# Third layer's norm, turn and rotation jobs inside its input tiles, a spare bank for the third up tile, and ScalarE copying both turned halves in the differential attention

## The reference, cut to what matters

```python
def diff_attn(q, k, v, lam):                       # layers 1 and 2 (first_block)
    s = jnp.einsum("bqhmd,bkhmd->bhmqk", q, k) * (B_QK_DIM ** -0.5)
    p = jax.nn.softmax(s, axis=-1)
    a = p[:, :, 0] - lam * p[:, :, 1]
    return jnp.einsum("bhqk,bkhd->bqhd", a, v)

def project(t):                                    # layer 3, in _even_mixer (second_block)
    qa, ka, va, qb, kb, vb = jnp.split(t @ w_in, EVEN_SPLITS, axis=-1)
    return (_rms_norm(_heads(qa, 8, 64), q_gain), _rms_norm(_heads(ka, 2, 64), k_gain), _heads(va, 2, 64), ...)
    # then qa = _rope(qa, cos, sin); ka = _rope(ka, cos, sin)

def _conv_ffn(h, w_up, conv_w, conv_b, w_down):    # all four layers (layers 1 and 2: conv_ffn)
    gate, val = jnp.split(h @ w_up, 2, axis=-1)
    gate = conv(gate, conv_w, width 3, per channel) + conv_b
    return (jax.nn.silu(gate) * val) @ w_down
```

## Time and profile before

| | us |
|---|---|
| median of 3 runs | 3829.44 (3820.06 to 3830.59) |
| profiled execution | 3837.57 |
| its span | 3835.8 |
| TensorE matmuls busy | 3506.9 (91%) |
| VectorE busy | 2035.1 (53%) |
| ScalarE busy | 1306.4 (34%) |
| POOL busy | 410.5 (11%) |

### The profile page before, as it was taken

The page is one execution under the profiler, slowest core; times in us unless marked ns, Lnnn a source line. Parts: engine busy times, 40 slices in busy tenths (PEclk is TensorE's granted clock), DMA queues, the critical chain, the costliest instruction groups (busy, mean ns, idle before and its releaser), DMA issues.

```text
span 3835.8 us, 47682 instructions
## 1 busy us (share of the span) xinstructions
PE 3506.9 (91%) x19065; PEld 2828.1 (74%) x19065; DVE 2035.1 (53%) x3250; ACT 1306.4 (34%) x1977; POOL 410.5 (11%) x351
## 2 busy tenths in 40 slices
PE   6997889999989888999997879899999879989998
PEld 5875678888868666787785547788888656667886
DVE  3655455635546655868413674474454355554354
ACT  4224332212233333323222552531221535434233
POOL 2003430000000140000001471000000013300000
PEclk8997889999999889999997999999999889999999
DMA  5430033434422102555320002134343211113332
GB/s 183 132 111 17 9 83 99 135 95 126 128 60 65 33 18 88 179 156 183 95 64 25 11 20 62 58 124 121 105 129 91 47 31 30 39 50 93 98 98 75
DMA packets 466715, 322.60 MB, mean 84 GB/s; under 512 B 51408, under 2 KB 439262, under 8 KB 466496
## 3 DMA queue, kind: packets, MB, share of 16 engines
q1 hardware_dynamic: 456864, 299.93, 26.2%
q0 software_dynamic: 9632, 19.62, 1.9%
HBM read 312.94 MB, written 4.55 MB: 83 GB/s over the span
## 4 chain that ended last, share of the span: by engine, by line
PE 82%; DVE 7%; ACT 5%; issue 3%; DMA 3%; POOL 1%; SPq 0%; DVEq 0%; ACTq 0%; POOLq 0%
PE PS L999 78%; PE PS L1320 3%; DMA RAW<-in_w_gate 2%; DVE CPROD L2485 1%; DVE TMP L2240 1%; ACT SPH L1582 1%; DVE ATT L2311 1%; DVE HL L2224 1%; ACT BIG L1766 1%; DMA RAW<-in_w_in 0%; DVE CACC L2565 0%; DMA XSTG<-in_x 0%; ACT PTR L1744 0%; DVE ML L2798 0%; DVE TMP L2785 0%
## 5 line engine op out<-in xcount | busy, mean ns | idle before, releaser
L999 PE MATMUL PS<-HH,SPH 128*128 128x512 f32 (+1 forms) x3424 | 1182.8, 358 | 87.1 <-ACT HH L1711 20.5
L999 PE MATMUL PS<-HL,SPH 128*128 128x512 f32 (+1 forms) x3424 | 1139.6, 356 | 4.6 <-DVE HL L2224 4.5
L999 PEld LDWEIGHTS PS<-HH,SPH 128*128 128x128 f32 x3424 | 657.6, 192 | 203.4 <-issue 84.6
L999 PE MATMUL PS<-HH,SPL 128*128 128x512 f32 (+1 forms) x3424 | 742.4, 356 | 0.0
L999 PEld LDWEIGHTS PS<-HL,SPH 128*128 128x128 f32 x3424 | 648.4, 192 | 95.3 <-DVE HL L2224 7.5
L2112 DVE TENSOR_TENSOR SPL<-RAW,SPH 128x1024 fp32r<-128x1024 f32 (+2 forms) x367 | 458.1, 1249 | 435.4 <-ACT SPH L1582 434.8
L999 PEld LDWEIGHTS PS<-HH,SPL 128*128 128x128 f32 x3424 | 583.4, 191 | 95.4 <-issue 4.0
L1582 ACT ACTIVATE SPH<-RAW 128x1024 fp32r<-128x1024 f32 (+2 forms) x367 | 393.9, 1074 | 721.3 <-PE PS L999 461.8
L999 PE MATMUL PS<-MH,SPH 128*128 128x512 f32 (+1 forms) x1056 | 362.7, 357 | 3.7 <-ACT SPH L1582 3.7
L999 PE MATMUL PS<-ML,SPH 128*128 128x512 f32 (+1 forms) x1056 | 360.6, 356 | 0.0
L2417 DVE SCALAR_TENSOR_TENSOR X<-PS,MOD,X 128x512 f32<-128x512 f32 (+1 forms) x144 | 95.3, 662 | 406.1 <-PE PS L999 404.1
(11 more groups left out here) (337 smaller groups left out, 3619.3 us busy)
## 6 DMA issues: line engine op xcount, KB each, us to landing
MS<-in_mod_turned SPq DMA_DIRECT2D x144, 512.0 KB, 3.4
RAW<-in_l_w_up SPq DMA_DIRECT2D x88, 512.0 KB, 3.9
RAW<-in_w_gate SPq DMA_DIRECT2D x44, 512.0 KB, 4.6
RAW<-in_w_val SPq DMA_DIRECT2D x44, 512.0 KB, 4.6
RAW<-in_w_down SPq DMA_DIRECT2D x32, 704.0 KB, 5.7
RAW<-in_l_w_down SPq DMA_DIRECT2D x32, 704.0 KB, 4.7
RAW<-in_w_in SPq DMA_DIRECT2D x40, 512.0 KB, 4.9
MS<-in_w_mod SPq DMA_DIRECT2D x32, 512.0 KB, 4.6
```

Source lines behind the costliest of these rows:

```text
L999: return pe.matmul(o, a, b, start=start, stop=stop)
```

## The change

It has three parts. In the third layer the turns, norms and rotations move into the tiles of `w_in`: the turns into tiles 2 to 5, and the chunks 4, 0, 1, 2, 3 one after another into tiles 6 to 12, each with its sums in one tile, its spread in the next and its rotation in the one after. The rotation's scratch is `big(5)` in place of `TMP[0]`, and `kv_in` is raised after the rotation of chunk 4. The third tile of each layer's first `up` goes to `AUX` in place of `LIN[0]` and doesn't wait on `tile_free`; with it, in all linear layers with lead tiles, the fourth tile is split in turn j = 1 in place of j = 2. In the differential attention ScalarE copies all turned parts.

```diff
+        def up_place(up, j, s):
+            return AUX if up.lead and j == 2 else LIN[s % 2]
+        QK_CHUNKS, QK_AT, VALUES_AT = (4, 0, 1, 2, 3), 6, {2: (0, 1), 3: (2,), 4: (3,), 5: (4,)}
...
-                            on_dve = k == (1 if self.mla else 0) or k == 2 and m % 2 == 0
+                            on_dve = not self.diff and (k == (1 if self.mla else 0) or k == 2 and m % 2 == 0)
...
-                if t >= 2:
+                if t >= 2 and not spare:
                     pe.wait_ge(S.tile_free, t if out is not None else t - 1)
-                out = LIN[slot] if out is None else out
+                out = AUX if spare else LIN[slot] if out is None else out
...
-                    linear(L["w_in"], HH, HL, None, S.h_ready)
+                    def qk_chunks(j):
+                        for i in VALUES_AT.get(j, ()):
+                            pe.wait_ge(S.tile_free, L["w_in"].t0 + i + 1)
+                            v = big(5) if i == 0 else VRAW[:, i - 1, :]
+                            turn_chunks([[(v[:, k * P:(k + 1) * P], P, slice(0, P)) for k in range(NTC)]])
+                        if j == QK_AT:
+                            turns_read()
+                        if 0 <= j - QK_AT - 2 < 5:
+                            rope((QK_CHUNKS[j - QK_AT - 2],))
+                        if 0 <= j - QK_AT - 1 < 5:
+                            broadcast(n0 + j - QK_AT - 1)
+                        if 0 <= j - QK_AT < 5:
+                            statistics(n0 + j - QK_AT, (QK_CHUNKS[j - QK_AT],))
+                    linear(L["w_in"], HH, HL, None, S.h_ready, mid=qk_chunks)
...
-                    turn_chunks([[(src[:, j * P:(j + 1) * P], P, slice(0, P)) for j in range(NTC)]
-                                 for src in [big(5)] + [VRAW[:, c, :] for c in range(4)]])
-                    turns_read()
-                    norm([(c,) for c in (4, 0, 1, 2, 3)], TOK, False, big, full=False)
-                    rope((4, 0, 1, 2, 3))
...
-                    linear(up, HH, HL, None, S.h_ready)
+                    linear(up, HH, HL, None, S.h_ready, spare=up.lead)
...
-                    if x.lead and j == 0:
+                    if x.lead and j < 2:
                         split_next(t + 1)
-                    elif t + 1 < n_tiles and not (x.lead and j == 1):
+                    elif t + 1 < n_tiles and not (x.lead and j == 2):
                         split_next(t)
...
-                    linear(L["w_in"], evac)
-                    read_turns([(VTG[:, :, :], NTC)], P)
-                    read_turns([(VTB[:, :, c * P:(c + 1) * P], NTC) for c in range(4)], P)
-                    norm([(c,) for c in (4, 0, 1, 2, 3)], TOK, big, 64, full=False)
+                        if 0 <= j + 1 - QK_AT < 5:
+                            square_single(big(QK_CHUNKS[j + 1 - QK_AT]), TOK)
+                    def early(j):
+                        for i in VALUES_AT.get(j, ()):
+                            read_turns([(VTG[:, :, :] if i == 0 else VTB[:, :, (i - 1) * P:i * P], NTC)], P)
+                        if 0 <= j - QK_AT < 5:
+                            act.wait_ge(S.sq_used, w.taken[S.sq_used])
+                            column_root(TOK, 64, False)
+                    linear(L["w_in"], evac, early)
...
-                    if x.lead and j == 0:
+                    if x.lead and j < 2:
                         split(t + 2, t % 2, kc_of[t + 2])
-                    elif t + 1 < n_tiles and not (x.lead and j == 1):
+                    elif t + 1 < n_tiles and not (x.lead and j == 2):
...
+                    def qk_chunks(j, t, s):
+                        if 0 <= j - QK_AT < 5:
+                            reciprocal(TOK, False)
+                        if 0 <= j - QK_AT - 1 < 5:
+                            apply_norm(gain, (QK_CHUNKS[j - QK_AT - 1],))
+                        if 0 <= j - QK_AT - 2 < 5:
+                            c = QK_CHUNKS[j - QK_AT - 2]
+                            dve.wait_ge(S.rope_landed, 48 * (li + 1))
+                            rope((c,), tmp=big(5))
+                            if c == 4:
+                                dve.wait_ge(*w.last)
+                                dve.memset(SM[:, 10:11], 0.0).then_inc(S.kv_in, w.one(S.kv_in))
+                    linear(L["w_in"], qk_chunks)
```

More of the change, by code:

```diff
@@ L999, in mm, with tile @@
                 return pe.matmul(o, a, b, start=start, stop=stop)
-            def tile(t, kc, toks, hi, lo, out=None, mid=None, chunk=None):
+            def tile(t, kc, toks, hi, lo, out=None, mid=None, chunk=None, spare=False):
                 slot = t % 2
                 pe.wait_ge(S.hi_ready, t + 1)
-                if t >= 2:
+                if t >= 2 and not spare:
                     pe.wait_ge(S.tile_free, t if out is not None else t - 1)
-                out = LIN[slot] if out is None else out
+                out = AUX if spare else LIN[slot] if out is None else out
                 for a, n in spans(toks):
@@ L1047, in lead, with linear @@
                             last.then_inc(S.tile_done, 1)
-            def linear(x, hi, lo, also=None, ready=None, order=range(DC), mid=None, chunk=None):
+            def linear(x, hi, lo, also=None, ready=None, order=range(DC), mid=None, chunk=None, spare=False):
                 def body(j, t, s):
@@ L1054, in body @@
                     else:
-                        tile(t, x.kc, x.toks[j], hi, lo, None, mid and (lambda: mid(j)), None if j else chunk)
+                        tile(t, x.kc, x.toks[j], hi, lo, None, mid and (lambda: mid(j)), None if j else chunk, spare and j == 2)
                     if also:
@@ L1194, in rs_read, with norm_parts @@
                     pe.wait_ge(S.inverse_ready, w.taken[S.inverse_ready])
-            def norm(groups, toks, center, chunk, full=True, summed=False):
-                rs_read()
+            def norm_parts(toks, center, chunk, full=True, summed=False):
                 def statistics(n, grp):
@@ L1235, in broadcast, with norm @@
                     last.then_inc(S.rs_done, w.one(S.rs_done))
+                return statistics, broadcast
+            def norm(groups, toks, center, chunk, full=True, summed=False):
+                rs_read()
+                statistics, broadcast = norm_parts(toks, center, chunk, full, summed)
                 n0 = w.made.get(S.rs_done, 0)
@@ L1649, in norm @@
                             act.wait_ge(S.centered, w.seen(S.centered))
[L1650 to L1655, removed]
+                        square_single(chunk(c), toks)
                     act.wait_ge(S.sq_used, w.taken[S.sq_used])
@@ L2169, in norm, with apply_norm @@
                         reciprocal(toks, full)
-                    dve.wait_ge(S.rs_done, w.seen(S.rs_done))
-                    apply(grp, RS)
-                    dve.wait_ge(*w.last)
-                    dve.memset(SM[:, 15:16], 0.0).then_inc(S.rs_free, w.one(S.rs_free))
+                    apply_norm(apply, grp)
+            def apply_norm(apply, grp):
+                dve.wait_ge(S.rs_done, w.seen(S.rs_done))
+                apply(grp, STAT)
+                dve.wait_ge(*w.last)
+                dve.memset(SM[:, 15:16], 0.0).then_inc(S.rs_free, w.one(S.rs_free))
             def center_chunks(T):
@@ L2693, in _ @@
                 elif l == 0:
-                    linear(L["w_in"], lambda j, t, s: None)
                     def gain(grp, RS):
@@ L2700, in gain @@
                             .then_inc(S.rope_in, w.one(S.rope_in))
-                    norm([(c,) for c in (4, 0, 1, 2, 3)], TOK, big, 64, gain, full=False)
-                    dve.wait_ge(S.rope_landed, 48 * (li + 1))
-                    rope((4, 0, 1, 2, 3))
+                    def qk_chunks(j, t, s):
[8 more added lines that the diff above has]
+                            if c == 4:
+                                dve.wait_ge(*w.last)
+                                dve.memset(SM[:, 10:11], 0.0).then_inc(S.kv_in, w.one(S.kv_in))
+                    linear(L["w_in"], qk_chunks)
                     dve.wait_ge(*w.last)
                     dve.memset(SM[:, 11:12], 0.0).then_inc(S.qk_ready, w.one(S.qk_ready))
-                    dve.wait_ge(*w.last)
-                    dve.memset(SM[:, 10:11], 0.0).then_inc(S.kv_in, w.one(S.kv_in))
                     dve.wait_ge(*w.last)
@@ L2771, in gate_or_val @@
                         dve.wait_ge(S.tile_done, t + 1)
-                        ps = LIN[s % 2]
+                        ps = up_place(up, j, s)
                         if j % 2 == 0:
```

23 lines of the change are left out of this document (16 added, 7 removed).

## The result

The changed kernel takes 3770.34 us (median of 4 runs, 3765.72 to 3772.88) against 3829.31 us (median of 4, 3820.06 to 3830.59) for the kernel before: ratio 0.985, 95% interval 0.9832 to 0.9868, so 57 us less, between 51 and 64. 3780 was forecast. In the profiled executions the span fell from 3835.8 to 3770.7 us, 65 us; the one before lay 8 us over its median, the one after 3.

What follows compares the result with a forecast made beforehand. TensorE, ending last for 82% of the span, was taken as the bound, so only its idle or low-clock time counted. 29.9 + 19.1 + 0 = 49.0 us off the median 3829.44 gave 3780 us, range 3768 to 3800.

Steps and rivals of the forecast that it cites:

- Part 1: Third layer, between `w_in` and attention: moving the jobs into the tiles gives 29.9 us, 28.5 plus 1.4 of clock.
- work moved in: Third layer's `w_in` tiles: TensorE still pays 23.75 us for the jobs, 19.35 plus 4.4 for transposes.
- the lower bound of 22.85: Third layer's `w_in` tiles: the moved work costs 19.35 + 3.5 us if transposes overlap the next weight load.
- ScalarE's signal: Behind the third layer's last `w_in` tile: only ScalarE's copy and signal remain before the first scores, 0.91 us.
- one attention step comes back to the full rate: Third layer's attention start: the first step costs 1.39 us less, then the lower clock again; 1.4 us taken.
- the first and the last rival: Third layer's `w_in`: jobs wait, 14 us less gain, chance 0.10; small matmuls drop TensorE to 1.2 GHz, 3866 us, chance 0.03.
- Part 2: Third up tile of each layer's first half in the spare bank: 19.1 us, bounds 11.4 and 21.7.
- The clock does come back: Third up tiles: without the stall the low clock goes, 7.7 us; the rival that it stays had chance 0.13.
- The new wait at the fourth tile: Second and fourth layers' up: reading the second tile stands behind the earlier splits, costing about 1.3 us each.
- Part 3: Differential attention: ScalarE copying both turned halves wins 0 us; bounds +2 and -17.5 us.
- +2 us (the last steps of a layer ...): Differential attention's last steps: halves were read in parallel and earlier VectorE work could help, at most 2 us.
- The other fear, that ScalarE would bound: Differential attention: ScalarE becomes the bound, 17.5 us less gain, 3798 us, chance 0.07.

Runs made afterwards that it cites:

- e1: The kernel before with only the third layer's turns, norms and rotations moved into the `w_in` tiles; 3801.99 us, ratio 0.9923.
- e10: The changed kernel with the third layer's norms and rotations starting at `w_in` tile 11 instead of 6; 3770.76 us, ratio 0.9838.
- e2: The kernel before with only the third up tile in the spare bank and the fourth tile's splits one turn earlier; 3817.53 us, ratio 0.9956.
- e11: The changed kernel with the spare bank also for the third tile of `w_out` (first two layers) and `w_in` (fourth layer); 3758.81 us, ratio 0.9811.
- e4: The changed kernel with VectorE's split for the fourth up tile back in its old turn, ScalarE's still early; 3771.03 us, ratio 0.9842.
- e9: The changed kernel with both engines' splits of the fourth tile back in their old turn, spare bank kept; 3767.37 us, ratio 0.9829.
- e3: The kernel before with only the differential attention's turned halves both copied by ScalarE; 3826.44 us, ratio 0.9983.
- e5: The changed kernel, but VectorE still copies one turned half per differential attention step; 3781.23 us, ratio 0.9872.
- e8: e5 with VectorE issuing the next round's copy one place earlier in the last rounds of differential attention; 3771.51 us, ratio 0.9855.

## Why the forecast was right, and where it was wrong

**Part 1** was forecast at 29.9 us and measured at 29.5 alone (ratio 0.9908 to 0.9938, which is 24 to 35) and at 29.1 by the shift of the splits. Its terms hold one by one. From the first to the last split of the third layer's `w_in` it is 151.9 us before and 175.7 after, 23.8 us of work moved in against 23.75 forecast (174.5 and 22.6 us in e1, which lies nearer to the lower bound of 22.85); a tile with three jobs takes 12.23 us; ScalarE's signal takes 0.90; one attention step comes back to the full rate and the second doesn't. No wait showed in the tiles, and TensorE ran at clock 1.00 through them, so the first and the last rival fall. e10 adds that neither the jobs' tile nor the DMAs had to be where they are.

**Part 2** was forecast at 19.1 us and measured at 16.9 (11.5 to 22.2). In e2 the four stretches from the first to the fifth up split give 5.4, 3.0, 5.8 and 3.4 us against 6.2, 3.4, 6.2 and 3.4. The clock does come back: the first layer's tile takes 8.46 us, not 10.71. With the stall the tile is slow, without it it isn't, here and again in e11 with the same two lead tiles ahead. This is the side of the Trainium skill's page "TensorE: Matmul & The Clock Gate", Part 1, that the forecast took, and the traces agree at these tiles. Behind the first attention they don't: there TensorE was busy 18.68 of 20 us and stayed at clock 0.50 (last section). The new wait at the fourth tile is there: 0.72 us of idle in the trace and 1.0 us by e4, against 1.3 forecast (the Silu that the second tile's reading needs had ended at 1469.07; VectorE stood with its split until 1470.05, for ScalarE's, and the reading came at 1471.19). That page's strict queues on VectorE agree too: the reading didn't pass the split.

**Part 3** is the step that failed: "20 us of work. But the maxima wait 16.1 us in sum for TensorE ... So nothing is won." The row is right, and the conclusion was drawn from one of two consumers. VectorE's queue releases TensorE in two places: the maxima lead to the next exponentials, and the copies lead to the values products. The maxima wait for TensorE throughout; the copies don't at the end of an attention, where the sequence written out by hand has them behind a subtraction that waits for GpSimd. The bound of "+2 us (the last steps of a layer ...)" named the place, but without a row for it. What stands in its place, from the means of the profiles with and without the wait in the table: 3.9 us in the first layer's stretch (13.56 against 9.70), 0.5 us in the second layer's steady steps, 1.4 us of idle at the second layer's end (3.06 against 1.70), and from the last values product to the first up split 94 us in four of five profiles with the wait, against 86 to 89 in the four without it in the table and in e4 and e10. Three terms are shown and make 5.8 us. The last one would add 3 to 5, but that the wait causes it is not shown: e2, with the wait, had 88.26, and e9, without it, 94.05. e3 alone measured 6.5 (1.9 to 11.1). The other fear, that ScalarE would bound, fell: moving the copies cost nothing that a trace shows.

**The sum** of 49.0 us without part 3 is what e5 measured, 0.9872, also 49.0 us (41 to 57). The whole gave 57 (51 to 64); the 8 us between are part 3, as far as two intervals that overlap can say. The medians, 3770 against 3780, differ by about that amount. That the range to 3768 held it is partly luck: it had 2 us for part 3, and the rest came from room that had been given to terms of parts 1 and 2.

## What to carry to other kernels

Before costing a move of work off an engine at nothing, list every consumer of what it makes, not only the one that the groups by line show waiting, and read the last steps of a loop apart from its middle: there the order written out for the middle puts ready work behind work that waits. Idle time booked to "issue" can be a real wait: look which instruction on another engine ended just before. Try the order in the queue first (e8): it gave what moving the work gave.

## What the runs showed that wasn't expected

TensorE can be busy and stay at the low clock. In the kernel before it was granted 0.50, that is 1.2 GHz, from 439.61 us on for 20.5 us, while busy 18.68 of 20 us. What came ahead of the fall was the end of the attention and the start of the norm, 10.24 us at the full clock, busy 7.16 of them, with no idle time over 1.44 us; the 2.52 us of idle lie further back. Every profile falls to the low clock at this place, and how long it lasts is what differs: mean granted clock from the last values product to the first up split 0.87 in the kernel before, 0.92 in the one after, 0.94 in e2, which had the 2.52 us, and 0.87 in e9, which hadn't and came into the norm with 37 us at clock 1.00 behind it. So the low clock there can cost 5 us or more, and what decides how long it lasts stays open.

One kernel differs from run to run by such draws. The kernel before lay between 3823.43 and 3841.18 us in 20 runs. e2's runs go from 3803.96 us at a mean clock of 0.959 to 3823.22 at 0.955. The third layer from its last `w_in` split to its third `w_out` split, where e3 changes nothing, takes 309.7 us in the profile before and 306.2 in e3's. A difference of 3 to 7 us in one stretch of two profiles is therefore no evidence by itself, as e3 showed of the 17 us that I had ascribed to part 3.
